# A streaming encoder's trunk on one core: rows of the experts' w2 are dealt to partitions in neighbouring pairs

## The reference, cut to what matters

```python
D_MODEL, SEQ, N_EXPERTS, TOP_K, EXPERT_FF = 1024, 256, 8, 2, 3584

def moe_swiglu(x, w_router, b_router, w1, w3, w2):
    t = x.reshape(b * s, d)
    logits = jnp.dot(t, w_router) + b_router
    top_val, top_idx = lax.top_k(logits, TOP_K)
    top_w = jax.nn.softmax(top_val, axis=-1)
    gates = jnp.sum(jax.nn.one_hot(top_idx, N_EXPERTS) * top_w[..., None], axis=1)
    out = jnp.zeros_like(t)
    for e in range(N_EXPERTS):
        he = jax.nn.silu(t @ w1[e]) * (t @ w3[e])      # (256, 3584)
        out = out + gates[:, e:e + 1] * (he @ w2[e])   # w2[e]: (3584, 1024)
    return out.reshape(b, s, d)
```

## Time and profile before

| | us |
|---|---|
| median of 3 runs | 1454.17 (1453.58 to 1457.19) |
| the profiled execution's own time | 1452.38 |
| its span, first to last instruction | 1450.6 |
| TensorE busy | 1376.1 (95%) |
| VectorE busy | 1137.1 (78%) |
| ScalarE busy | 956.2 (66%) |
| transposes of `e_h`, line 938, 224 of them | 29.7 busy |
| 336 DMAs of expert weights, issue to landing | 5.4 each (median) |

### The profile page before, as it was taken

One profiled execution on the slowest core, in us unless ns is written; L12 is line 12 of the kernel. 1 busy time (PEld: TensorE's weight loads), 2 busy tenths in 40 slices (PEclk: granted clock), 3 DMA queues, 4 the chain that ended last, 5 costly groups with the idle time before them and its releaser, 6 DMA issues.

```text
span 1450.6 us, 18772 instructions
## 1 busy us (share of the span) xinstructions
PE 1376.1 (95%) x7014; PEld 1177.8 (81%) x7015; DVE 1137.1 (78%) x927; ACT 956.2 (66%) x817; POOL 34.8 (2%) x53
## 2 busy tenths in 40 slices
PE   6888999998878999999999999999999999999997
PEld 5677999988767888888788888878888888888886
DVE  5666644446766888988888898889899889888986
ACT  5655433436774777777677777677777777777774
POOL 4200000000000000000000000000000000000000
PEclk9889999999997999999999999999999999999999
DMA  6409665543542999999899999989999989999970
GB/s 235 145 1 349 207 197 176 172 140 123 176 145 87 343 375 372 359 368 363 308 369 375 373 351 375 364 306 368 377 348 374 372 337 347 368 377 355 375 276 31
DMA packets 142530, 415.65 MB, mean 287 GB/s; under 512 B 6995, under 2 KB 39888, under 8 KB 142432
## 3 DMA queue, kind: packets, MB, share of 16 engines
q1 hardware_dynamic: 141856, 414.22, 78.1%
q0 software_dynamic: 576, 0.11, 0.1%
HBM read 413.26 MB, written 1.05 MB: 286 GB/s over the span
## 4 chain that ended last, share of the span: by engine, by line
PE 85%; DVE 7%; ACT 4%; issue 3%; POOL 1%; DMA 0%; DVEq 0%; SPq 0%; ACTq 0%; POOLq 0%
PE ps L592 27%; PE ps L594 26%; PE ps L593 26%; PE ps L938 2%; PE ps L905 1%; DVE w_lo L1769 1%; ACT w_hi L1296 1%; PE ps L629 1%; DVE w_lo L1365 1%; PE ps L917 1%; PE ps L919 1%; DVE xb_conv L1644 0%; DVE expert_in_lo L1749 0%; POOL head_sumsq L570 0%; DMA residual<-in_x_dram 0%
## 5 line engine op out<-in xcount | busy, mean ns | idle before, releaser
L1769 DVE TENSOR_TENSOR w_lo<-w_raw,w_hi 128x2048 fp32r<-128x2048 f32 x333 | 759.8, 2290 | 112.2 <-ACT w_hi L1296 109.3
L1296 ACT ACTIVATE w_hi<-w_raw 128x2048 fp32r<-128x2048 f32 x333 | 638.0, 1919 | 249.0 <-PE ps L594 249.0
L592 PE MATMUL ps<-w_hi,expert_in_hi 128*128 128x512 f32 x896 | 352.2, 393 | 5.2 <-issue 3.5
L594 PE MATMUL ps<-w_hi,expert_in_lo 128*128 128x512 f32 x896 | 349.1, 390 | 0.0
L593 PE MATMUL ps<-w_lo,expert_in_hi 128*128 128x512 f32 x896 | 348.8, 389 | 0.0
L592 PEld LDWEIGHTS ps<-w_hi,expert_in_hi 128*128 128x128 f32 x896 | 168.3, 188 | 41.3 <-issue 4.3
L594 PEld LDWEIGHTS ps<-w_hi,expert_in_lo 128*128 128x128 f32 x896 | 168.2, 188 | 35.3
L593 PEld LDWEIGHTS ps<-w_lo,expert_in_hi 128*128 128x128 f32 x896 | 168.3, 188 | 33.8
L592 PE MATMUL ps<-w_hi,expert_hT_hi 128*128 128x512 f32 x448 | 174.8, 390 | 0.0
L594 PE MATMUL ps<-w_hi,expert_hT_lo 128*128 128x512 f32 x448 | 174.4, 389 | 0.0
L593 PE MATMUL ps<-w_lo,expert_hT_hi 128*128 128x512 f32 x448 | 174.4, 389 | 0.0
(11 more groups left out here) (316 smaller groups left out, 1236.4 us busy)
## 6 DMA issues: line engine op xcount, KB each, us to landing
w_raw<-in_moe_w_dram SPq DMA_DIRECT2D x336, 1024.0 KB, 5.4
w_raw<-in_ffn_w_dram SPq DMA_DIRECT2D x33, 1024.0 KB, 5.5
w_raw<-in_lru_w_in_dram SPq DMA_DIRECT2D x8, 1024.0 KB, 5.3
w_raw<-in_mla_w_o_dram SPq DMA_DIRECT2D x4, 1024.0 KB, 5.4
w_raw<-in_lru_w_out_dram SPq DMA_DIRECT2D x4, 1024.0 KB, 4.9
w_raw<-in_mla_w_in_dram SPq DMA_DIRECT2D x4, 704.0 KB, 8.2
w_raw<-in_mla_w_qb_dram SPq DMA_DIRECT2D x3, 768.0 KB, 4.3
w_raw<-in_mla_w_kvb_dram SPq DMA_DIRECT2D x2, 1024.0 KB, 9.3
```

What stands on the lines that cost most here:

```text
L592: pe.matmul(dst, a[0], b[0], start=start, stop=False)
L594: return pe.matmul(dst, a[1], b[0], start=False, stop=stop)
L1296: act.activation(w_hi[hi_slot(N_PRE + u)][:], raw[slot][:], ACT.Copy).then_inc(hi_ready, 1)
L1769: dve.tensor_tensor(w_lo[s][:], raw[s][:], w_hi[h][:].bitcast(F32), ALU.subtract).then_inc(lo_ready, 1)
```

## The change

In SP's `one_pass` the pattern of a w2 unit becomes `"o (p k) n -> p (o k) n"`: partition p receives rows 2p and 2p + 1 of the unit's 256, which are neighbours in memory (8 KB in one piece), and not rows p and 128 + p. w1 and w3 keep their pattern. So that each row still meets its column of `e_h`, `turn` no longer turns 128 neighbouring columns: block c takes, of the 256 columns that unit c // 2 of w2 covers, every second one, beginning with column c % 2. The columns of the stationary operand then lie 8 bytes apart. The numbers of DMAs, of transposes, of matmuls and of waits stay as they are, and so does their order.

```diff
@@ -494,7 +494,8 @@
                     sp.wait_ge(unit_used, base + (d * N_BODY + N_PRE + u - RAW_SLOTS + 1))
-                    sp.dma_start(dst, src.rearrange("o (k p) n -> p (o k) n", p=P)).then_inc(raw_landed[slot], 16)
+                    rows_first = "o (p k) n -> p (o k) n" if name == "w2" else "o (k p) n -> p (o k) n"
+                    sp.dma_start(dst, src.rearrange(rows_first, p=P)).then_inc(raw_landed[slot], 16)
@@ -935,7 +936,8 @@
                     for c in range(MCOLS[t][1] // P):
-                        ins = pe.transpose(ps[:, 6 + c // 4, c % 4 * P:(c % 4 + 1) * P], e_h[:, c * P:(c + 1) * P], ident[:])
+                        pair = e_h[:, c // 2 * 2 * P:(c // 2 + 1) * 2 * P].rearrange("p (m k) -> p k m", k=2)
+                        ins = pe.transpose(ps[:, 6 + c // 4, c % 4 * P:(c % 4 + 1) * P], pair[:, c % 2, :], ident[:])
```

## The result

The changed kernel takes 1458.55 us (median of 20 runs, 1455.38 to 1462.26), the kernel before 1454.65 (20 runs, 1452.75 to 1457.19). The ratio is 1.0024, 95% interval 1.0018 to 1.0030: 2.6 to 4.4 us slower. That is clear of no change, and within the 0.3% that the prediction had set as its bound. The profiled execution took 1457.18 us, 4.80 over that of before.

The account below looks back on a forecast made before the run. TensorE was taken as the bound, with no engine waiting for loads. 1452.4 us profiled + 0 for loads + 0 for transposes = 1452.4, carried over 1454.2 us; own range 1450 to 1458, range given 1450 to 1479.

Parts of the forecast that it names:

- What bounds the kernel: TensorE, busy 95% of the span; ACT's 285 waits ahead of `w_hi` all end on TensorE, none on a DMA.
- the loads go unseen: w2 loads in 8 KB runs: 0 us, unless such runs are 27% slower.
- The rival in which DMA is the bound: w2 units load at 431 GB/s: 1418 us at the least, 1436 with half of that; chance 0.06.
- Packets: DMA packets of the whole span fall by 14,336, from 142,530 to about 128,200.
- The transposes: Line 938, 224 transposes with loaded columns 8 bytes apart: taken as 0, bounds 0 to +24.4 us.
- the row of step 0: Line 847 loads one column 128 times in 190 ns, neighbouring columns take 191; taken to show column placement costs nothing.
- the point from which it would decide: Gap cost at line 938 decides from 19 ns for each transpose, distance 109 ns becoming 129; 4.4 us in all.
- within 0.3%: Kernel time stays within 4.4 us, what a measurement can tell from no change; chance 0.82.
- the rival: Line 938's weight load: the gap in the loaded columns costs up to +24.4 us, 1478.6 us; chance 0.10.
- The argument by the rate of bytes: A load with gaps spans 9.4 bytes a ns, hardly more than the 9.0 of a streamed matmul operand.
- Its other reading: Each crossing into a new 16-byte line pays; twice the crossings at the transposes, sum near +24.4 us.
- What would show it: Signs: fewer packets, eight transposes at 0.87 us, loads 140 ns, period 246.4 us; 1.0 us or more means the slower rival.

Follow-up runs that it names:

- the loads alone: Changed kernel with transposes back on neighbouring columns, only w2's 8 KB runs kept; against the kernel before 1455.43 us beside 1454.89, ratio 1.0003.
- the second deal: Changed kernel, transposes on neighbouring columns; silu and product read PSUM at every second column, write `e_h` in neighbours; against the kernel before 1454.49 us beside 1455.33, 0.9997.
- step 8: Transposes load every eighth column (every fourth in the last chunk), w2 in 4 KB runs; against the kernel before ratio 1.0006.
- step 1: Transposes load neighbouring columns, as in the kernel before; 109 ns between transposes, ratio 1.
- step 2: Transposes load every second column, w2 in 4 KB runs; against the kernel before 1459.54 us beside 1454.89, ratio 1.0035.
- step 4: Transposes load every fourth column, w2 in 4 KB runs; against the kernel before ratio 1.0025.

## Why the prediction was right, and where not

*What bounds the kernel*: right. TensorE, and ACT's 285 waits for it, are unchanged; "the loads go unseen" was borne out by the loads alone, 1.0003. The rival in which DMA is the bound and 8 KB runs make it faster would have shown in that run and in the second deal (0.9997), and did not. By the Trainium skill's 358 GB/s ("DMA: Bandwidth & Descriptors", Specifications) the loads would bound the kernel before and after alike. The trace does not agree: the changed kernel moves 374 GB/s in 530 to 560 us, over that figure again, and its 285 waits end on TensorE.

*Packets*: right to the unit, 14,336 fewer.

*The transposes*: here the step failed. "I take 0, by the row of step 0" was mis-sized: the term is 24 x 0.08 us for the turns of eight, 8 x 0.03 for those of four and 32 x 0.02 behind the turns, 2.8 us. The bounds held (0 to 24.4), and so did the point from which it would decide, 19 ns for 0.3%; 11 ns stay under it, which is why "within 0.3%" came true although the loss is real. That is luck: no row of before said 11 ns and not 20. The mechanism was the rival's, at a ninth of its highest price. The row of step 0 could not carry the 0: a load that reads one column 128 times says nothing of a load that walks (the column at line 847 is moreover one of the identity, not of a bias), and 190 and 191 ns are records, which step 8 showed to be no price. The argument by the rate of bytes, 9.4 against 9.0 a ns, is refuted too: step 8 spans 4096 bytes in 0.110 us, 37 bytes a ns, and is as fast as step 1.

The Trainium skill's rule of two hits on a 16-byte line ("SBUF — State Buffer", "Door 1: The DMA port swizzle") made step 2 free. The trace does not agree: step 2 costs 11 ns, step 4 with one hit a line about the same (11 to 13 ns), and step 8 nothing or 1 ns. Its other reading, that each crossing pays, which was put near +24.4 us, is as far off.

*What would show it*: I had named 0.87 us for no cost and 1.0 for the rival, and left out the stretch between, where the answer lay. The loads' record, said to stay at 140 ns, is 209, and the period of the loop, said to stay at 246.4 us, is 247.06. The median of 1458.55 also leaves the forecast's own range, 1450 to 1458, and by 0.05 us the mark of 1458.5 from which I had called myself wrong; 0.45 us of that is the kernel before, whose 20 runs have 1454.65 and not 1454.2. Only the wide range, opened up to 1479 for the load with gaps, holds it.

## What to carry to other kernels

A layout that makes DMA runs longer is worth nothing where no engine waits for a landing; ask that first, and only then what the other side of the layout pays. If a permutation has to be somewhere, try the places at the same total: a read of PSUM at every second column by ScalarE and VectorE was free here, while `e_h` walked in jumps doubled ScalarE's instruction and made VectorE's 1.7 times as long, and a weight load with gaps made a transpose 10% dearer on the engine that bounds the kernel. Slack is a matter of the engine's queue, not of the instruction: the product had 2.9 to 13.5 us until its reader, and made TensorE wait through what was queued behind it.

## What the runs showed of the hardware that I had not expected

The distance between transposes depends on the step of the loaded float32 columns in no simple order: about 109, 120, 116, 121, 135, 123 and 109 ns for steps 1, 2, 3, 4, 6, 7 and 8. A transpose between two 512-column matmuls delays them by some 116 ns, more than the 109 in a row of eight. ScalarE's and VectorE's time for 1024 columns is the same (1.01 and 1.21 us) for PSUM read at step 1 and 2, but 2.08 and 2.09 when neighbouring results go to places 512 bytes apart in SBUF (and VectorE also reads one operand there in the same order).
